# Twelve projection panels with the weights stationary and the tokens streaming

## The reference

```python
proj = einsum('bsd,de->bse', x, w_in)            # 2048 -> 4*1024 + 8 + 6*512 columns
(q, k, v, g_att, fg, c_b, c_c, c_h, g_conv, p_u, g_pool) = split(proj)
y_att  = forgetting_attention(q, k, v, fg, b_f) * silu(g_att)      # 8 heads of 128
y_conv = c_b * causal_conv3(c_c * c_h, conv_w) * silu(g_conv)
y_pool = pool_mixer(p_u, pool_w, pool_scale) * silu(g_pool)        # windows 2, 4, 8, 16
x = layer_norm(ALPHA * x + concat(y_att, y_conv, y_pool) @ w_out)
# second block: h = x + gated linear attention; + swiglu; + gate * (p @ w_ple); rmsnorm
```

## Time and profile before

| what | value |
|---|---|
| median of 3 runs | 1728.8 us |
| span of the profiled execution | 1727.2 us |
| PE busy | 1705.6 us, 99% of the span |
| PEld busy | 1401.8 us, 81% |
| DVE busy | 1025.0 us, 59% |
| ACT busy | 802.1 us, 46% |
| DMA | 315.46 MB, 183 GB/s mean |
| PE's share of the chain that ended last | 96% |
| share of 16 DMA engines that the hardware queue's packets took | 56.6% |

### The profile page before, as it was taken

How to read it: one execution, slowest core, us unless ns; L and a number is a source line. 1 busy time by engine, 2 the same in 40 slices (tenths; PEclk the granted TensorE clock), 3 DMA queues, 4 the chain that set the end, 5 groups by cost and what they waited for, 6 DMA issues and landing times.

```text
span 1727.2 us, 21748 instructions
## 1 busy us (share of the span) xinstructions
PE 1705.6 (99%) x7827; PEld 1401.8 (81%) x7827; DVE 1025.0 (59%) x1085; ACT 802.1 (46%) x967; POOL 99.4 (6%) x95
## 2 busy tenths in 40 slices
PE   8999999999999999999999999999999999999997
PEld 6888877888777888877888888888888888888886
DVE  4444465566755899955555455455465465565755
ACT  4444444444456555545444443443434444444653
POOL 6000000000110122210000000000000000000001
PEclk9999999999999999999999999999999999999999
DMA  8566645666464644555656566666566666656553
GB/s 258 158 188 184 183 146 147 219 209 215 149 199 134 177 147 152 157 165 180 218 183 190 188 192 191 188 190 191 189 189 191 190 188 192 191 187 194 180 184 133
DMA packets 160175, 315.46 MB, mean 183 GB/s; under 512 B 9772, under 2 KB 11888, under 8 KB 159216
## 3 DMA queue, kind: packets, MB, share of 16 engines
q1 hardware_dynamic: 158480, 304.12, 56.6%
q0 software_dynamic: 1632, 10.46, 1.6%
HBM read 310.36 MB, written 4.19 MB: 182 GB/s over the span
## 4 chain that ended last, share of the span: by engine, by line
PE 96%; DVE 2%; DMA 1%; ACT 1%; issue 0%; POOL 0%; POOLq 0%; DVEq 0%; SPq 0%; ACTq 0%
PE acc L588 29%; PE acc L590 29%; PE acc L589 29%; PE aux L604 2%; PE aux L745 2%; DMA w_raw<-in_w_out 1%; DVE w_lo L1248 1%; PE aux L811 0%; PE aux L637 0%; PE aux L758 0%; PE aux L759 0%; PE aux L636 0%; ACT w_hi L937 0%; DVE h_tok L1478 0%; PE aux L729 0%
## 5 line engine op out<-in xcount | busy, mean ns | idle before, releaser
L1248 DVE TENSOR_TENSOR w_lo<-w_raw,w_hi 128x1024 fp32r<-128x1024 f32 x572 | 704.9, 1236 | 584.7 <-ACT w_hi L937 584.1
L937 ACT CAST w_hi<-w_raw 128x1024 fp32r<-128x1024 f32 x572 | 599.9, 1051 | 821.3 <-PE acc L590 796.6
L588 PE MATMUL acc<-w_hi,a_hi 128*128 128x512 f32 x1664 | 658.6, 396 | 3.0 <-DVE w_lo L1248 3.0
L590 PE MATMUL acc<-w_hi,a_lo 128*128 128x512 f32 x1664 | 650.2, 391 | 0.0
L589 PE MATMUL acc<-w_lo,a_hi 128*128 128x512 f32 x1664 | 649.7, 390 | 0.0
L588 PEld LDWEIGHTS acc<-w_hi,a_hi 128*128 128x128 f32 x1664 | 313.7, 189 | 72.9 <-issue 10.3
L590 PEld LDWEIGHTS acc<-w_hi,a_lo 128*128 128x128 f32 x1664 | 313.4, 188 | 66.5
L589 PEld LDWEIGHTS acc<-w_lo,a_hi 128*128 128x128 f32 x1664 | 313.9, 189 | 62.8 <-issue 0.2
L588 PE MATMUL acc<-w_hi,act_hi 128*128 128x512 f32 x320 | 124.6, 389 | 0.0
L590 PE MATMUL acc<-w_hi,act_lo 128*128 128x512 f32 x320 | 124.5, 389 | 0.0
L589 PE MATMUL acc<-w_lo,act_hi 128*128 128x512 f32 x320 | 124.5, 389 | 0.0
(11 more groups left out here) (236 smaller groups left out, 887.9 us busy)
## 6 DMA issues: line engine op xcount, KB each, us to landing
w_raw<-in_ffn_w_in SPq DMA_DIRECT2D x176, 512.0 KB, 3.4
w_raw<-in_w_in SPq DMA_DIRECT2D x112, 512.0 KB, 3.6
w_raw<-in_gla_w_in SPq DMA_DIRECT2D x96, 512.0 KB, 3.9
w_raw<-in_ffn_w_out SPq DMA_DIRECT2D x88, 512.0 KB, 3.6
w_raw<-in_w_out SPq DMA_DIRECT2D x32, 512.0 KB, 4.7
w_raw<-in_gla_w_out SPq DMA_DIRECT2D x32, 512.0 KB, 3.6
w_raw<-in_ple_w_gate SPq DMA_DIRECT2D x32, 512.0 KB, 3.9
x_tok<-in_x SPq DMA_DIRECT2D x8, 256.0 KB, 8.7
```

What stands on the lines that cost most here:

```text
L588: pe.matmul(banks[t][:], hi[:, k + c, tok], wh, start=st, stop=False)
L590: mm = pe.matmul(banks[t][:], lo[:, k + c, tok], wh, start=False, stop=en)
L937: nc.scalar.copy(w_hi[u % RING][:], w_raw[u % RING][:]).then_inc(hi_done, 1)
L1248: nc.vector.tensor_tensor(w_lo[u % RING][:], w_raw[u % RING][:], w_hi[u % RING][:], ALU.subtract).then_inc(lo_done, 1)
```

## The change

A new function `turned_unit` takes the place of `unit` in the twelve panels that are not values. It makes 128 x 128 pieces of the weights stationary and streams all 256 tokens: two chunks x four column blocks x three products = 24 matmuls of 256 columns a unit, where there were 12 of 512. Over twelve panels of eight units that is 2304 in place of 1152. The result has features on partitions; two column blocks share an `acc` bank, 256 columns each. `stage`, its copies on ACT and the 96 transposes go, and the `t` jobs leave the rotation of `aux` banks. The readers take their input from `acc`: ACT in the panel's own last unit, DVE in unit 0 of the next panel, behind that unit's `low` (for the last panel, 13, in unit 1 of the output projection). The values' panels and all other products keep `unit`.

```diff
--- before.py
+++ after.py
@@ -95,14 +95,12 @@
             u = p * UPP + j
             if (p, j) == (1, 0):
                 order.append(("fg", 0))
-            if j == 1 and p >= 1 and p - 1 not in (PV, PV + 1):
-                order += [("t", 2 * (p - 1)), ("t", 2 * (p - 1) + 1)]
             if (p, j) == (1, 6):
                 order.append(("ci", 0))
             if (p, j) == (13, 3):
                 order += [("pool", 0), ("pool", 1)]
             order += head_jobs(u)
-    order += [("t", 2 * PPG), ("t", 2 * PPG + 1), ("pt", 0)]
+    order.append(("pt", 0))
     order += [("hn", i) for i in range(UPP)]
     for g in range(NPG * UPP):
         order += [(name, i) for name, i in gla_jobs(g)]
...
@@ -590,6 +587,24 @@
                         mm = pe.matmul(banks[t][:], lo[:, k + c, tok], wh, start=False, stop=en)
                 mm.then_inc(unit_used, 1)
 
+            def turned_unit(u, p, hi, lo, k, first, last):
+
+                pe.wait_ge(lo_done, u + 1)
+                if first and p >= 2:
+                    panel_read(pe, p - 2)
+                banks = panel_banks(p)
+                for c in range(UNIT):
+                    st, en = first and c == 0, last and c == UNIT - 1
+                    for blk in range(N // P):
+                        half = blk % 2
+                        o = banks[blk // 2][:, half * TOK:(half + 1) * TOK]
+                        wh = w_hi[u % RING][:, c, blk * P:(blk + 1) * P]
+                        wl = w_lo[u % RING][:, c, blk * P:(blk + 1) * P]
+                        pe.matmul(o, wh, hi[:, k + c, :], start=st and half == 0, stop=False)
+                        pe.matmul(o, wh, lo[:, k + c, :], start=False, stop=False)
+                        mm = pe.matmul(o, wl, hi[:, k + c, :], start=False, stop=en and half == 1)
+                mm.then_inc(unit_used, 1)
+
             def begin(name, i=0):
 
                 _, bank, turn = job(name, i)
...
@@ -609,13 +624,6 @@
-
-            def turn_stage(p):
-
-                panel_read(pe, P_IN + p)
-                for i in range(2):
-                    b = begin("t", 2 * p + i)
-                    turn_tiles(stage[p % 2], b, 2 * i * P).then_inc(aux_done, 1)
@@ -661,7 +669,8 @@
                     u = U_IN + p * UPP + j
                     if p == 0:
                         job_read(pe, "x", j)
-                    unit(u, P_IN + p, a_hi, a_lo, 2 * j, j == 0, j == UPP - 1)
+                    shape = unit if p in (PV, PV + 1) else turned_unit
+                    shape(u, P_IN + p, a_hi, a_lo, 2 * j, j == 0, j == UPP - 1)
                     if p == 0 and j < UPP - 2:
                         turn_x(2 + j)
                     if (p, j) == (0, UPP - 1):
@@ -672,8 +681,6 @@
-                    if j == 1 and p >= 1 and p - 1 not in (PV, PV + 1):
-                        turn_stage(p - 1)
@@ -699,8 +706,6 @@
-                if j == 1:
-                    turn_stage(PPG)
@@ -969,45 +974,20 @@
...
-            tanhs = [0]
...
-            def gate_tanh(i):
...
-                job_done(act, "t", i)
-                if tanhs[0] >= 2:
...
-                nc.scalar.activation(tanh[i % 2][:].rearrange("p k t -> p (k t)"), bank_of("t", i)[:], ACT.Tanh,
-                                     scale=0.5).then_inc(tanh_done, 1)
-                tanhs[0] += 1
...
+            def gate_tanh(p):
...
+                before = {PGA + 1: PGA, PCG: PGA + 1, PPG: PCG}.get(p)
+                for i, b in enumerate(panel_banks(P_IN + p)):
+                    if before is not None:
+                        panel_read(act, P_IN + before, i + 1)
+                    nc.scalar.activation(tanh[i][:].rearrange("p k t -> p (k t)"), b[:], ACT.Tanh,
+                                         scale=0.5).then_inc(tanh_done, 1)
...
-                    if j == 1 and p >= 1:
-                        q = p - 1
-                        for i in (2 * q, 2 * q + 1):
-                            src = bank_of("t", i)[:].rearrange("p (k t) -> p k t", t=TOK) if ("t", i) in JOB else None
-                            if q in (PQ, PQ + 1):
...
-                                nc.scalar.activation(qT[:, 2 * i:2 * i + 2, :], src, ACT.Copy,
-                                                     scale=float(P) ** -0.5).then_inc(read_of("t", i), 1)
...
-                            if q in (PGA, PGA + 1, PCG):
-                                gate_tanh(i)
...
@@ -1039,18 +1019,32 @@
...
-                        if p >= 2 and ("t", 2 * (p - 2)) in JOB and p not in (PV, PV + 1):
...
-                            job_done(act, "t", 2 * (p - 2) + 1)
-                        dst = v_tok[:, :, (p - PV) * N:(p - PV + 1) * N] if p in (PV, PV + 1) else stage[p % 2]
-                        stage_panel(P_IN + p, dst)
+                        if p in (PV, PV + 1):
+                            stage_panel(P_IN + p, v_tok[:, :, (p - PV) * N:(p - PV + 1) * N])
+                        if p in (PQ, PQ + 1, PCC, PPU):
+                            panel_done(act, P_IN + p)
+                            if p == PCC:
+                                act.wait_ge(zeros, 2)
+                            if p == PPU:
+                                act.wait_ge(zeros, 1)
+                            for i, b in enumerate(panel_banks(P_IN + p)):
+                                src = b[:].rearrange("p (k t) -> p k t", t=TOK)
+                                if p in (PQ, PQ + 1):
+                                    k = 4 * (p - PQ) + 2 * i
+                                    turned = nc.scalar.activation(qT[:, k:k + 2, :], src, ACT.Copy, scale=float(P) ** -0.5)
+                                if p == PCC:
+                                    turned = nc.scalar.copy(convu[:, 2 * i:2 * i + 2, 2:], src)
+                                if p == PPU:
+                                    turned = nc.scalar.copy(poolu[:, 2 * i:2 * i + 2, PAD:], src)
+                                turned.then_inc(acc_read[(P_IN + p) % 2], 1)
+                        if p in (PGA, PGA + 1, PCG, PPG):
+                            panel_done(act, P_IN + p)
+                            gate_tanh(p)
...
-                    gate_tanh(2 * PPG)
-                    gate_tanh(2 * PPG + 1)
...
@@ -1280,13 +1274,14 @@
...
-            def gate(i, dst):
-
-                gates[0] += 1
-                dve.wait_ge(tanh_done, gates[0])
-                nc.vector.scalar_tensor_tensor(dst, tanh[i % 2][:], 1.0,
-                                               bank_of("t", i)[:].rearrange("p (k t) -> p k t", t=TOK),
-                                               ALU.add, ALU.mult).then_inc(read_of("t", i), 1)
+            def gate(p, dst):
+
+                for i, b in enumerate(panel_banks(P_IN + p)):
+                    gates[0] += 1
+                    dve.wait_ge(tanh_done, gates[0])
+                    nc.vector.scalar_tensor_tensor(dst[:, 2 * i:2 * i + 2, :], tanh[i][:], 1.0,
+                                                   b[:].rearrange("p (k t) -> p k t", t=TOK),
+                                                   ALU.add, ALU.mult).then_inc(acc_read[(P_IN + p) % 2], 1)
...
@@ -1345,32 +1340,32 @@
...
-                    if j == 1 and p >= 1:
-                        q = p - 1
-                        for i in (2 * q, 2 * q + 1):
...
-                            if q in (PK, PK + 1):
...
-                                nc.vector.tensor_copy(kT[:, 2 * (i - 4):2 * (i - 4) + 2, :], src).then_inc(read_of("t", i), 1)
...
                     attention(u)
                     if u >= 4:
                         low(u + RING)
+                    if j == 0 and p >= 1:
+                        q = p - 1
+                        if q in (PK, PK + 1, PCH, PCB):
+                            panel_done(dve, P_IN + q)
+                            if q == PCH:
+                                panel_read(dve, P_IN + PCC)
+                            if q == PCB:
+                                panel_read(dve, P_IN + PCG)
+                            for i, b in enumerate(panel_banks(P_IN + q)):
+                                src = b[:].rearrange("p (k t) -> p k t", t=TOK)
+                                k = 4 * (q - PK) + 2 * i
+                                h = slice(2 * i, 2 * i + 2)
+                                if q in (PK, PK + 1):
+                                    turned = nc.vector.tensor_copy(kT[:, k:k + 2, :], src)
+                                if q == PCH:
+                                    turned = nc.vector.tensor_tensor(convu[:, h, 2:], src, convu[:, h, 2:], ALU.mult)
+                                if q == PCB:
+                                    turned = nc.vector.tensor_tensor(convg[:, h, :], src, convg[:, h, :], ALU.mult)
+                                turned.then_inc(acc_read[(P_IN + q) % 2], 1)
+                        if q in (PGA, PGA + 1):
+                            gate(q, gaT[:, 4 * (q - PGA):4 * (q - PGA) + 4, :])
+                        if q == PCG:
```

(66 more changed lines are left out.)

## The result

The changed kernel takes 1731.9 us (median of 15 runs, 1728.0 to 1733.6), the kernel before 1728.2 us (median of 15, 1725.5 to 1729.8). The ratio is 1.0018, with a 95% interval of 1.0010 to 1.0025: slower by some 3 us, where 9 us faster was forecast, and above the range's high end of 1729.

The account below looks back on a forecast made before the run. PE, busy 99% of the span, was taken as the bound, so only its own stream counts. Transposes -10.8 us and products +1.6 us sum to -9.2 us: 1728.8 to 1719.6 us, range 1716 to 1729.

Parts of the forecast that it names:

- Transposes removed: On PE's path in the twelve turned panels: 96 transposes, 12 turnings at 0.90 us each, save 10.8 us.
- The products: Twelve panels: 1152 matmuls at 226.7 ns (261.1 us) become 2304 at 114.0 ns (262.7 us), +1.6 us.
- The gate-rank product: Existing product with 32 columns loaded, 113.8 ns a matmul, taken as the nearest row for the new step of 114.0 ns.
- The forget-gate product: Existing product with 8 columns loaded, 116.7 ns a matmul; as the new step it would make the products +7.8 us.
- The break-even at 118.0 ns: Step of the new matmuls at which the 10.8 us gain from removed transposes is used up.
- The load just fits: New matmuls on PE: a load takes about 111 ns and a stream 113, so it hides with 2 ns to spare.
- The rival in which the load becomes the bound: New matmuls: handing over adds 10 ns to the load's 111.6, step 121.6 ns, +8.3 us, 1737 us; chance 0.13.
- The rival of the unsettled stream: New matmuls stay slow after interruptions, step 117 to 118 ns, gain used up, 1726 to 1729 us; chance 0.20.
- Loads that aren't hidden at all: Each new matmul costs stream and load, 224 ns: +255 us, some 1973 us; chance 0.01.
- Taking the results out at no cost: Reads of results on ACT and DVE, moved to new places, stay covered and cost PE nothing.
- Elsewhere: Rest of the kernel, chiefly low granted clock after the layer norm: nothing in the sum, +-2 us on the range.
- the signs named: Profile after: starts 0.113 to 0.116 us apart, turned panel 21.7 to 22.2 us, panel 7 at 21.76, 1056 more loads.

Follow-up runs that it names:

- only_no_turning: Kernel after the change, but all 14 panels keep the old 512-column matmuls and nothing is turned; 1718.3 us, ratio 0.9941.
- widths: Kernel after the change with streamed columns varied by panel from 128 to 512, loads kept at 128 x 128; ran once, 1762.9 us, only its steps are read.
- loads: Kernel after the change with 32 to 120 loaded columns in panels 1 to 5, other product order in 12, operands swapped in 13; ran once, 1728.4 us.
- before_filled: Kernel before the change with six plain float32 matmuls put into PE's two waits behind the layer norm; 1726.2 us, ratio 0.9985.

## Why the prediction was wrong

**Transposes removed, -10.8 us: right.** 10.8 us to the mark in `only_no_turning`, 10.8 again from panel 1 on.

**The products, +1.6 us: wrong, and this is the step that failed.** "Half of 226.7 is 113.3" took the time of 512 columns as a rate. `widths` shows that it is 213.3 + 13.3: the columns and a fixed cost that doubles with the count of matmuls. 1152 more of them at 13.3 ns are 15.3 us where the sum has 1.6; 13.8 were measured to the mark, less than 15.3 since the old stream had slow steps to lose. The gate-rank product seemed to confirm the rate, with 113.8 ns for 256 columns, but `loads` shows 113.3 for small loads and 120.0 for a full one. The sentence that a load of 128 columns doesn't slow the stream rested on comparing two numbers that differ in two things, columns streamed and columns loaded, whose effects happened to cancel. The forget-gate product's 116.7, also 256 columns behind a tiny load, was a warning of a cost beside the rate; why 8 loaded columns leave it there no run tested. The break-even at 118.0 ns was right but for those slow steps, and 120.0 lies above it.

The Trainium skill's "TensorE: Matmul & The Clock Gate", under "Back-to-back issue gap", gives a step at the full clock the form columns / 2.4 plus a constant, 2.5 ns there. The prediction noted that 226.7 is 11 ns over that page's figure and dropped the page. The trace disagrees with its constant, 13.3 for this kind of operand, but its form holds from 256 columns up, and with the constant read from rows 4, 226.7 - 213.3, it gives 106.7 + 13.3 = 120.0 ns: the measured step.

**The load just fits: right.** Behind short streams the step is 112 ns in `widths` (111.6 forecast for the load), below the stream's 120. The rival in which the load becomes the bound gave q = 121.6, near the measured 120.0, and 1737 us, 5 over the measured time; its mechanism is another: the addition is there, but on the stream, at 512 columns as at 256. The rival of the unsettled stream (117 to 118) named the wrong cause too; in a panel without small products every step of the new stream is 120 ns. Loads that aren't hidden at all did not occur; the sentence of the Trainium skill from which the prediction took that rival stands in that page's section "The mechanism", not in the one named.

**Taking the results out at no cost: right.** No wait of PE on `acc` behind a reader; the two kinds of waits on `acc` are for `w_lo`, 2.8 us in all where it was 3.1.

**Elsewhere, nothing in the sum and +-2 us: mis-sized.** The runs of the changed kernel spread over 5.6 us. Filling the two waits halves that, to 2.8 us, and takes 3.3 us off the median; of what is left, panel 0 alone varies by about one. The two stretches that the prediction read hold 2.1 us of loss, but the clock is low in those next to them as well, 6.8 us at half rate in all. That is up to 3.4 us lost, and `before_filled` takes 3.3 us less from the mark to the end than the kernel before.

Of the signs named, the first did not come (starts 0.120 us apart, a turned panel of 23.04 us, over the 22.7 that it named); PE's waits, panel 7 and the 1056 more loads came as forecast, and so did the 24 fewer operations of ACT.

## What to carry to other kernels

A step read at one width is not a rate: before a count of matmuls is changed at constant work, read the step at two widths with the same load, and split it into columns and a constant. Here the constant was 13 ns, 6% of a 512-column matmul and 11% of one with 256. Where a layout saves transposes by halving the width of a stream, set the constant times the added matmuls against them: 12 more a unit, eight units, at 13.3 ns are 1.28 us a panel, and eight transposes are 0.90.

And where TensorE must wait a few microseconds between dense stretches, it can pay to put matmuls into the wait that nobody needs, no longer than the wait itself: here six of them kept the clock up and made the otherwise unchanged kernel 0.15% faster.

## What the runs showed of the hardware that was not expected

The fixed cost of an fp32r matmul behind a full load: 13.3 ns at 256, 320, 384 and 512 columns (12 at 272 and 288, 16 at 448), with a floor of 112 ns under it at 128, 192 and 240. It falls to 7 to 10 ns at 256 columns when 32 to 120 are loaded, with 96 (115.8 ns) worse than 112 (113.3), and does not fall at 384 or 512. Alternating widths behind equal loads (512 and 256) cost 3 ns a matmul over the sum of their parts. And one program's granted clock took different courses, 3.4 us at the lower level with a span of 1727.7 us and 10.2 with 1731.6.
